# Joints between products rebuilt: roots on four columns, two tiles fed input by input, stages joined in blocks

## The reference

```python
def _rmsnorm(x, w):
    xf = x.astype(jnp.float32)
    y = xf * lax.rsqrt(jnp.mean(xf * xf, axis=-1, keepdims=True) + EPS)
    return (y * w.astype(jnp.float32)).astype(x.dtype)

def _conv_ffn(h, w_up, conv_w, w_down):
    u = _causal_dwconv(jnp.matmul(h, w_up), conv_w)
    gate, val = jnp.split(u, 2, axis=-1)
    return jnp.matmul(jax.nn.silu(gate) * val, w_down)
```

## Time and profile before

| | us |
|---|---|
| median of 3 runs | 2762.54 (2760.06 to 2762.85) |
| profiled execution, its own time | 2768.55 |
| its span, first to last instruction | 2766.7 |
| TensorE busy (matmuls) | 2431.3 (88%) |
| VectorE busy | 1773.5 (64%) |
| ScalarE busy | 674.2 (24%) |
| GpSimd busy | 208.1 (8%) |

### The profile page before, as it was taken

The page is one execution under the profiler, slowest core; times in us unless marked ns, Lnnn a source line. Parts: engine busy times, 40 slices in busy tenths (PEclk is TensorE's granted clock), DMA queues, the critical chain, the costliest instruction groups (busy, mean ns, idle before and its releaser), DMA issues. The chain is left out here.

```text
span 2766.7 us, 33416 instructions
## 1 busy us (share of the span) xinstructions
PE 2431.3 (88%) x13390; PEld 1938.0 (70%) x13390; DVE 1773.5 (64%) x2721; ACT 674.2 (24%) x1229; POOL 208.1 (8%) x175
## 2 busy tenths in 40 slices
PE   4998867798999989699979997799996997799996
PEld 3885755686788878487655575688784785588785
DVE  6663663764788865527787867566667784666644
ACT  2212332102121100411467722222202112222200
POOL 1001330200100001000031000000010001000000
PEclk9998985899999999899989998899998998899998
DMA  4220001241233345322210044233363452233341
GB/s 151 77 76 1 3 2 46 77 145 38 76 99 99 93 144 168 107 61 69 61 61 1 2 165 147 69 94 97 118 211 105 170 196 69 58 95 99 118 130 56
DMA packets 68314, 252.75 MB, mean 91 GB/s; under 512 B 7584, under 2 KB 7872, under 8 KB 67392
## 3 DMA queue, kind: packets, MB, share of 16 engines
q1 hardware_dynamic: 67584, 248.35, 28.1%
q10 hardware_dynamic: 576, 2.28, 0.2%
HBM read 248.50 MB, written 2.10 MB: 91 GB/s over the span
## 5 line engine op out<-in xcount | busy, mean ns | idle before, releaser
L305 PE MATMUL psum<-rounded_n,rounded_high 128*128 128x512 f32 x1856 | 741.5, 400 | 70.5 <-PEq L404 46.8
L306 PE MATMUL psum<-rounded_n_low,rounded_high 128*128 128x512 f32 x1856 | 730.1, 393 | 0.0
L307 PE MATMUL psum<-rounded_n,rounded_ring 128*128 128x512 f32 x1856 | 729.9, 393 | 0.0
L305 PEld LDWEIGHTS psum<-rounded_n,rounded_high 128*128 128x128 f32 x1856 | 354.4, 191 | 154.6 <-issue 80.0
L282 DVE CAST rounded_high<-ring 128x1024 fp32r<-128x1024 f32 (+1 forms) x360 | 244.6, 680 | 323.7 <-PE psum L307 312.3
L284 DVE TENSOR_TENSOR rounded_ring<-ring,rounded_high 128x1024 fp32r<-128x1024 f32 (+1 forms) x360 | 440.9, 1225 | 12.4
L306 PEld LDWEIGHTS psum<-rounded_n_low,rounded_high 128*128 128x128 f32 x1856 | 354.1, 191 | 77.6 <-issue 4.3
L307 PEld LDWEIGHTS psum<-rounded_n,rounded_ring 128*128 128x128 f32 x1856 | 353.1, 190 | 75.2
L305 PE MATMUL psum<-rounded_hid_high,rounded_high 128*128 128x512 f32 x528 | 207.8, 394 | 14.3 <-PEq L1934 14.3
L306 PE MATMUL psum<-rounded_hid_low,rounded_high 128*128 128x512 f32 x528 | 207.3, 393 | 0.0
L307 PE MATMUL psum<-rounded_hid_high,rounded_ring 128*128 128x512 f32 x528 | 207.0, 392 | 0.0
(11 more groups left out here) (445 smaller groups left out, 3291.9 us busy)
## 6 DMA issues: line engine op xcount, KB each, us to landing
ring<-in_w_up SPq DMA_DIRECT2D x132, 512.0 KB, 3.5
ring<-in_w_down SPq DMA_DIRECT2D x48, 512.0 KB, 3.5
n_low<-in_mod_w SPq DMA_DIRECT2D x48, 512.0 KB, 4.8
ring<-in_w_ab_in SPq DMA_DIRECT2D x37, 512.0 KB, 3.6
ring<-in_w_mix_in SPq DMA_DIRECT2D x31, 512.0 KB, 3.6
z<-in_mod_w SPq DMA_DIRECT2D x24, 512.0 KB, 6.0
ring<-in_w_sc_in SPq DMA_DIRECT2D x24, 512.0 KB, 4.8
mod_room<-in_mod_w SPq DMA_DIRECT2D x24, 512.0 KB, 5.6
```

The lines of the kernel that those rows point to most:

```text
L305: self.nc.tensor.matmul(out, w_high, x_high, start=(k0 + k == 0), stop=False)
L306: self.nc.tensor.matmul(out, w_high, x_low, start=False, stop=False)
L307: last = self.nc.tensor.matmul(out, w_low, x_high, start=False, stop=(k0 + k == kt - 1))
```

## The change

1. **Stages joined.** A `Stage` holds one function for each engine; `together` makes one block of several stages, each engine running their functions one after the other. up_0, down_0, ab_norm and ab_in are one block; ab_out, ffn_norm_1, up_1, down_1, sc_norm, sc_in, sc_out, ffn_norm_2, up_2, down_2, last_norm and the store are another. What a block's end ordered is ordered by semaphores: a down product waits for each hidden tile (`inputs_ready`) and for the banks of the product before it (`banks_free`); the modulation loads and those of ab_in wait on SP until the product before is done.
2. **`lead`.** The first two output tiles of up_1, up_2, sc_in and ab_in are computed together: for each input tile k, a wait for it, then three matmuls for each of the two tiles. The wait is on the low part of that input (`done` of the edge before).
3. **`edge` in place of `boundary`.** Squares are summed over features by matmuls that have the squares as weights and one column of ones as the moving operand, so that the sums of 512 tokens lie in 128 partitions by four columns (in four banks). The root and the reciprocal are of four columns. They are spread back to all partitions by four matmuls, with each column broadcast to 128 as weights and the identity as moving operand. VectorE reads the reciprocal from PSUM. The last square tile goes to TensorE directly; GpSimd adds the first seven. VectorE splits the third weight piece of the next product ahead of the first reciprocal.
4. **Smaller edits.** `plain_product` squares from PSUM before it copies; the root's table is loaded at the start of the product (`load_root_table`); the output is stored tile by tile as h is renewed; the clearing block between ffn_norm_1 and up_1 now stands between the sparse attention and ab_out; buffers of the later stages share one arena.

```diff
+def together(k, *stages):
+    with k.nc.Block() as block:
+        @block.tensor
+        def _(pe):
+            for stage in stages:
+                if stage.tensor is not None:
+                    stage.tensor(pe)
...
-    def product(self, pe, name, rhs, width, evacuated, between=None, inputs_ready=None):
+    def product(self, pe, name, rhs, width, evacuated, between=None, inputs_ready=None, lead=1, banks_free=None):
         n_out, kt = PRODUCTS[name]
-        i = self.first_tile[name]
-        for j in range(n_out):
+        first, chunks = self.first_tile[name], self.chunks(name)
+        for j in range(lead if lead > 1 else 0):
+            if banks_free is not None:
+                pe.wait_ge(banks_free[0], banks_free[1] - PRODUCT_BANKS + j + 1)
+            pe.wait_ge(self.weights_split, first + j + 1)
+        for k in range(kt if lead > 1 else 0):
+            if inputs_ready is not None:
+                pe.wait_ge(inputs_ready, k + 1)
+            for j in range(lead):
+                last = self.passes(self.psum[:, j % PRODUCT_BANKS, 0:width], first + j, k, rhs(k), k == 0, k == kt - 1)
+                if k == kt - 1:
+                    last.then_inc(self.weights_used, 1)
+        for j in range(lead if lead > 1 else 0, n_out):
...
+def edge(k, name, before, first_gain, gain=None, shift=None, then=None, y=None):
...
+    def spread_root(pe, i):
+        pe.wait_ge(inverted, i + 1)
+        for c in range(TT):
+            last = nc.tensor.matmul(k.psum[:, SPREAD + i, c * P:(c + 1) * P],
+                                    k.roots[:, i, c:c + 1].broadcast_to([P, P]), k.const("ident"),
+                                    start=True, stop=True)
+        last.then_inc(spread, 1)
+
+    def tensor(pe):
+        pe.wait_ge(added, KT - 1)
+        for c in range(TT):
+            nc.tensor.matmul(k.psum[:, SUMS + c, 0:1], k.sum_sq[:, c * P:(c + 1) * P], one, start=True, stop=False)
+        pe.wait_ge(squared, KT)
+        for c in range(TT):
+            last = nc.tensor.matmul(k.psum[:, SUMS + c, 0:1], k.squares[:, (KT - 1) % 2, c * P:(c + 1) * P], one,
+                                    start=False, stop=True)
+        last.then_inc(summed, 1)
+        spread_root(pe, 0)
+        if gain is None:
+            return
+        for j in range(KT):
+            pe.wait_ge(resquared, j + 1)
+            for c in range(TT):
+                last = nc.tensor.matmul(k.psum[:, SUMS + c, 1:2], k.squares[:, j % 2, c * P:(c + 1) * P], one,
+                                        start=(j == 0), stop=(j == KT - 1))
+            last.then_inc(counted, 1)
+        spread_root(pe, 1)
...
+    def invert(dve, i):
+        dve.wait_ge(rooted, i + 1)
+        nc.vector.reciprocal(k.roots[:, i, :], k.roots[:, i, :]).then_inc(inverted, 1)
+        dve.wait_ge(spread, i + 1)
+        return k.psum[:, SPREAD + i, :]
+
+    def vector(dve):
+        link = Link(dve, steps)
+        if then is not None:
+            k.split_weights(dve, then, 0)
+        rstd = invert(dve, 0)
+        dve.wait_ge(out, KT)
+        for j in range(KT):
+            dst = k.h if y is None else y
+            step = nc.vector.scalar_tensor_tensor(dst[:, j, :], dst[:, j, :], first_gain[:, j:j + 1], rstd,
+                                                  ALU.mult, ALU.mult)
...
         first, chunks = k.first_tile[name] + RING, k.chunks(name)
+        sp.wait_ge(k.weights_used, k.first_tile[name])
+        if self.after is not None:
+            sp.wait_ge(self.after.used, self.after.n)
         sp.dma_start(self.cond, k.dram["cond"]).then_inc(self.cond_loaded, 16)
...
+            k.product(pe, name, rhs, T, out, inputs_ready=before.signals["hid_done"],
+                      banks_free=(before.signals["out"], before.signals["n_out"]))
...
+    def sync(sp):
+        for j in range(KT):
+            sp.wait_ge(before.signals["renewed"], j + 1)
+            sp.dma_start(k.dram["out"][:, j, :], k.h[:, j, :]).then_inc(k.stored, 16)
+        sp.wait_ge(k.stored, 16 * KT)
```

More of the change, by code:

```diff
@@ L299, in product @@
                 for k in range(n):
+                    kk = c * SLOT_KT + k
                     if j == 0 and inputs_ready is not None:
[L301 to L305, removed]
@@ L352, in _, with add_squares @@
                                         ALU.subtract).then_inc(done, 1)
[L355 removed]
+def add_squares(k, pool, squared, added, width=T, tiles=KT):
     nc = k.nc
[L358 removed]
+    for j in range(tiles):
         pool.wait_ge(squared, j + 1)
@@ new lines, in edge @@
+    squared, added, out = (before.signals[s] for s in ("squared", "added", "out"))
+    summed, rooted, inverted, spread, renewed, resquared, counted, scaled, shifted, steps, done = (
+        k.sem(f"{name}_{s}") for s in ("summed", "rooted", "inverted", "spread", "renewed", "resquared", "counted",
+                                       "scaled", "shifted", "steps", "done"))
+    SUMS, SPREAD = 4, 2
+    one = k.const("ones")[:, 0:1]
+    def spread_root(pe, i):
[5 more added lines that the diff above has]
+        last.then_inc(spread, 1)
@@ L2074, in mod_part, with pool, vector @@
+    def pool(pool):
+        add_squares(k, pool, squared, added, tiles=KT - 1)
+    def vector(dve):
+        for j in range(-1, KT):
+            k.split_weights(dve, name, j)
+            if mod is not None and j >= 0:
+                mod.sums(dve, j)
+        if mod is not None:
+            mod.finish(dve)
+    return Stage(sync, tensor, scalar, vector, pool, squared=squared, added=added, out=out)
 def mod_part(k, i, part):
@@ new lines, in build @@
+        norm = edge(k, "ab_norm", down, k.vec("final_norm"), mod_part(k, 0, 1), mod_part(k, 0, 0), "ab_in")
+        together(k, up, down, norm, ab_front(k, norm))
+        idle = k.high[:, :, :, :].rearrange("p a b x -> p (a b x)")
+        per = TT * (TT + 1) // 2 * P
+        k.sel_bias = [[idle[:, a * per + i * (i + 1) // 2 * P:a * per + (i + 1) * (i + 2) // 2 * P]
+                       for i in range(TT)] for a in range(2)]
+        k.pt = k.n
+        k.rows = k.scratch
+        sparse_attention(k)
@@ new lines, in build @@
+        down_1 = plain_product(k, "down_1", k.hidden, k.n, mod, up_1)
+        norm_2 = edge(k, "sc_norm", down_1, mod_part(k, 0, 5), mod_part(k, 1, 1), mod_part(k, 1, 0), "sc_in", k.n)
+        mod = Modulation(k, "sc_in", 64, 24, 1, *modulation_room(k.hid_high[:, KT + 1:2 * KT + 1, :]), after=mod)
+        short = short_conv_mixer(k, mod, norm_2)
+        short_out = plain_product(k, "sc_out", k.hidden, k.n, before=short)
+        norm_3 = edge(k, "ffn_norm_2", short_out, mod_part(k, 1, 2), mod_part(k, 1, 4), mod_part(k, 1, 3), "up_2", k.n)
@@ new lines, in build, with tiles_of @@
+        up_2 = ffn_up(k, 2, norm_3)
+        mod = Modulation(k, "down_2", 88, 8, 1, *modulation_room(k.n_low), after=mod)
+        down_2 = plain_product(k, "down_2", k.hidden, k.n, mod, up_2)
+        norm_4 = edge(k, "last_norm", down_2, mod_part(k, 1, 5), y=k.n)
+        together(k, mixed, norm_1, up_1, down_1, norm_2, short, short_out, norm_3, up_2, down_2, norm_4,
+                 store_output(k, norm_4))
+    return k
+def tiles_of(k, first, n):
+    return k.arena[:, first * T:(first + n) * T].rearrange("p (a x) -> p a x", x=T)
@@ L3015, in modulation_room, with tail @@
+def tail(k, first, n):
+    return k.arena[:, 45 * T + first:45 * T + first + n]
 def modulation_room(room):
```

1535 lines of the change are left out of this document (749 added, 786 removed).

## The result

The changed kernel takes 2675.19 us (median of 4, 2675.07 to 2675.79) against 2762.69 for the one before (median of 4): ratio 0.9685, 95% interval 0.9668 to 0.9701, 87.5 us less. Forecast were 2669 and a range of 2655 to 2702. The profiled execution took 2675.26 us with a span of 2673.4. One run of experiment 5, at 2884.5 us and a mean granted clock of 0.818, was in a slower state and enters no figure.

A forecast was written before the change was run, and what follows sets the result against it. Products set their own pace; what is left are the joints between them. 36.6 + 20.2 - 2.3 + 6.4 + 26.9 + 4.0 + 1.4 = 93.2 us off 2762.54 gave 2669 us; range 2655 to 2702.

The forecast's parts named there:

- A: Joints into up_1, sc_in, up_2, ab_in: two tiles run as inputs get ready, start 9.15 us earlier, gain 36.6 us.
- E: Four up-to-down joints (sc_in to sc_out included): without a barrier the gaps close, gain 26.9 us.
- F: End of the kernel: output stored by tiles while VectorE still works, gain 4.0 us.
- C: Joints: squares of renewed tiles summed by eight one-column instructions a tile, 1.33 us at half clock, cost 2.3 us.
- D: Second root in four joints: root, reciprocal and spreading take 2.5 us instead of 4.1, gain 6.4 us.
- B: First root of the five joints on four columns: first rescaling comes sooner after the last matmul, gain 20.2 us.
- number 2: Joints: small matmuls don't overlap with their weight loads, 0.5 us each, so the kernel gets slower, 2788 us; 3 in 100.
- Rival 5: TensorE stays at the high clock in the joints: about 13 us more gain, 2656 us; 10 in 100.
- Rival 1: The two tiles fed input by input run at the low clock, some 8 us a joint lost, 2701 us; 10 in 100.
- G: Clearing block moved behind the sparse attention: TensorE idles there too, but fewer names are cleared, gain 1.4 us.

The follow-up runs named there:

- experiment 5: Changed kernel with the first root on four columns, but squares summed by 512-column matmuls and second root 512 columns wide: 2664.93, 2665.24 and 2674.70 us, ratio 0.9654.
- Experiment 2: Changed kernel with one output tile instead of two fed input by input: 2682.61 us, ratio 0.971.
- 3: Changed kernel with a barrier between each up (and sc_in) and the down behind it: 2710.54 us, ratio 0.9803.
- 11: Changed kernel with one 2 MB store behind the last tile instead of eight of 256 KB: 2679.63 us, ratio 0.9695.
- 4: Changed kernel with the roots as before: sums by 512-column matmuls, root and reciprocal over 512 columns, nothing spread: 2680.83 us, ratio 0.9699.
- warm: Changed kernel with 512-column matmuls whose result nobody reads put in TensorE's waits in the joints: 2681.22 us, ratio 0.9701.
- 6: Changed kernel with squares of the renewed tiles rounded and summed in one pass, 32 matmuls a joint instead of 64 instructions: 2675.32 us, ratio 0.9687.
- experiment 12: Changed kernel with one-pass squares, arena address kept, plus 512-column filler matmuls only where TensorE is free: 2651.32 us, ratio 0.9603.

## Why the prediction was right, and which term was off

The mechanisms came out as forecast: joints of 25 to 27 us instead of 36 to 44 (I had given 22 to 26), waits for the first input, no gap between up and down, transfers ending 2.4 us behind VectorE. Six of seven terms were within 3.1 us of their measured sizes; A, E and F were each confirmed by undoing them alone or in part (2, 3, 11), C and D together in 4 and 5.

**The mis-sized term is C**, "8 x 0.167 = 1.33 us at half clock", so "they fit beside it". They measured 0.216 us, 1.73 us a tile against 1.39 from VectorE; TensorE became the one that paces the squares in all four joints, not only in ab_norm, and C cost 13.0 us instead of 2.3. The 0.167 was a misreading of the earlier trace rows: a stretch of 1 us counts every instruction that overlaps it, those begun earlier too, so 6 in a stretch is fewer than 6 per us. The starts of that row in the trace of before are 0.112 us apart at clock 1.00 and 0.213 at 0.50: the right price was on hand. The total of a long unbroken row (13.81 / 64) gives it too. B had used the same wrong price for the closing sums (1.33 us) and got away with it, because there the clock was still high and they took 1.05. My closest rival, number 2, turned the sign at 0.43 us an instruction; the measured price is half of that, so the sign was never near. (It also counted 48 instructions around the two roots of a joint; the timeline shows four groups of eight, 32.)

What the price is, from start to start: 0.112 us at clock 1.00 (L482, and the squares in warm; a whole row of eight comes to 0.105 each, the figure of my expectations), 0.213 at 0.50, the same in two passes of one column and in one pass of two (6), so it goes by the number of instructions. The Trainium skill, page "TensorE: Matmul & The Clock Gate", section "LDWEIGHTS (loading the stationary operand)", gives a weight load as the number of its columns divided by 1.2, in ns: for 128 columns 107 ns. The spacing in the trace is near that at clock 1.00 (112 ns) and twice that at 0.50 (213 ns). That the load is what is paid was not tried by itself.

**The clock.** I had it low in the squares, as it was. Rival 5 (it stays high) was wrong for the changed kernel; experiment 12 shows what a higher clock is worth on top of the one-pass squares. Rival 1 (low through all 48 matmuls of the two tiles) was wrong: the clock rose 3.2 to 4.6 us after the product began, and the waits between inputs that were to hold it down didn't come. In up_1 TensorE, slow at first, fell behind the inputs and ran without a pause:

```profile
1708.90:1718.60 9.70, 9.70 (x44) 8.02 (x43) 5.37 (x9) 3.67 (x6) 0.00 (x0) 1.00 0.01 2
```

The rule of the Trainium skill that I had set beside it ("TensorE: Matmul & The Clock Gate", section "A second HAM failure mode: psum-queue depth-cycling") speaks of short idle times between groups of matmuls, so this kernel was no case of it. Experiment 2 had such idle times, about a third of a us before each of three inputs, and there too the clock stayed at 1.00.

**B and E** were 2.1 and 3.1 us larger than forecast, and most of B was not the four columns (4). Four of five first rescalings came 0.2 to 0.9 us earlier than I had them; in three of these four the first spread still ran at the high clock, 1.16 us instead of 2.08. In E I had put the ideal stretch at the instruction count times 0.228; the pace of after is 0.2267, 0.0013 x (3 x 528 + 192) = 2.3 us less. **F**: 6.2 less 2.4 is 3.8, not the 4.0 of the sum; it measured 4.5.

**The forecast's 6 us** over the median: 93.2 - 87.5 = 5.7, made of C (-10.7), B and E (+5.2), A, D and G (-1.2), F (+0.5), the unchanged code (+1.2), and 0.7 between the spans and the medians. That it came this close is in part luck: half of C's error was made up by terms that had been set too low.

## What to carry to other kernels

Many matmuls of one or two columns with 128x128 weights are paid by the instruction, in one pass or two; price them by the spacing in an unbroken row at the clock that they will have, and hold that against the pace of what feeds them. A rebuild that shortens one step (a reciprocal from 3.35 to 0.17 us) can hand the gain to the step between. Measure its halves apart: here the roots gave 15 us in the joints (9.4 and 5.9) and the squares took 13 back. After any edit that adds a tile compare the pace of untouched products too.

## What the runs showed of the hardware

- An unused tile of 8 bytes ahead of the arena moved its start from a multiple of 2048 bytes to 32 bytes past one. The rounded matmuls of 512 columns that read their moving operand there went from 0.2267 to 0.2333 us apart, at a granted clock of 1.00; 2160 of them come to 14 us, and 14.8 were measured. Other distances than 32 bytes weren't tried, nor the weights' address.
- With fillers of 512 float32 columns between the small matmuls (0.94 us a pair) the clock stayed at 1.00 in the joints that add h (warm); without them, and with fillers of 256 columns, it went to 0.50.
- A rescaling that reads its root from PSUM takes 0.75 us, no more than from SBUF.
